# Transposed activations split straight out of PSUM in four places, the norm of twelve heads moved, and the last chunk of the attention output projection taken piece by piece

## The reference, cut to what matters

```python
# first block: attention (differential and latent heads), then a gated convolution FFN
x = x + g1 * (_merge_heads(o_da, o_mla, subln_w, lambda_init) @ w_o)      # 256x2048 @ 2048x2048
h2 = _modulate(_rmsnorm(x, norm2_w), sh2, s2)
x = x + g2 * _conv_ffn(h2, w_up, conv_w, conv_b, w_down)
x = _rmsnorm(x, final_w)
# second block, layer 0: 16 delta-rule heads and 8 windowed heads side by side
proj = rmsnorm(x, norm_w[0]) @ hyb_w_in
o_a = gated_delta_chunked(q_a, k_a, v_a, beta, g)                          # 256 x 16 x 128
o_a = o_a * rsqrt(mean(o_a * o_a, -1) + EPS) * dn_norm_w                   # a norm for each head
y_a = o_a.reshape(256, 2048) * silu(az)
y_b = dilated_attention(q_b, k_b, v_b).reshape(256, 1024) * silu(bz)
x = x + concatenate([y_a, y_b], -1) @ hyb_w_out                            # 256x3072 @ 3072x2048
# layer 1: gated short convolution
gate_b, gate_c, u, z = split(rmsnorm(x, norm_w[1]) @ sc_w_in, 4)
x = x + (gate_b * causal_conv(gate_c * u) * silu(z)) @ sc_w_out
return rmsnorm(x, final_norm_w)
```

## Time and profile before

| | us |
|---|---|
| median of 3 runs | 3053.97 (3048.46 to 3054.05) |
| profiled execution | 3045.87 |
| its span | 3044.0 |
| PE busy | 2877.8 (95%) |
| DVE busy | 1813.1 (60%) |
| ACT busy | 1206.1 (40%) |
| POOL busy | 174.5 (6%) |

### The profile page before, as it was taken

How to read it: one execution, slowest core, us unless ns; L and a number is a source line. 1 busy time by engine, 2 the same in 40 slices (tenths; PEclk the granted TensorE clock), 3 DMA queues, 4 the chain that set the end, 5 groups by cost and what they waited for, 6 DMA issues and landing times.

```text
span 3044.0 us, 35020 instructions
## 1 busy us (share of the span) xinstructions
PE 2877.8 (95%) x13848; PEld 2353.2 (77%) x13848; DVE 1813.1 (60%) x2037; ACT 1206.1 (40%) x1210; POOL 174.5 (6%) x344
## 2 busy tenths in 40 slices
PE   6899998899999999998999999989689999999998
PEld 3597865677888888887877888878677888888887
DVE  2486777775565545565555668957754554455554
ACT  2232226444544334354344434424334344344333
POOL 0000314000000000000000000026200000000000
PEclk9999999999999999999899999999899999999999
DMA  9698974574654565556357767674146454655554
GB/s 393 240 335 284 339 266 143 197 274 149 207 183 168 196 219 177 193 170 192 136 173 257 226 222 234 207 229 117 46 142 199 167 193 161 212 193 193 175 168 155
DMA packets 348289, 618.60 MB, mean 203 GB/s; under 512 B 51808, under 2 KB 102640, under 8 KB 340864
## 3 DMA queue, kind: packets, MB, share of 16 engines
q1 hardware_dynamic: 311280, 583.88, 57.0%
q10 hardware_dynamic: 36880, 32.94, 3.2%
HBM read 587.76 MB, written 29.00 MB: 203 GB/s over the span
## 4 chain that ended last, share of the span: by engine, by line
PE 81%; DVE 10%; DMA 3%; ACT 2%; issue 1%; SPq 1%; POOL 1%; ACTq 0%; DVEq 0%; POOLq 0%
PE ps L309 21%; PE ps L311 20%; PE ps L310 20%; DVE w_lo L271 3%; PE ps L1098 3%; PE ps L1100 3%; PE ps L1099 3%; DVE upd L2435 1%; PE ps L1380 1%; ACT w_hi L264 1%; PE ps L692 1%; DMA g_row<-in_w_ada 1%; DVE w_lo L869 1%; PE ps L415 1%; PE ps L2733 1%
## 5 line engine op out<-in xcount | busy, mean ns | idle before, releaser
L271 DVE TENSOR_TENSOR w_lo<-raw,w_hi 128x2048 fp32r<-128x2048 f32 (+3 forms) x428 | 892.5, 2094 | 695.1 <-ACT w_hi L264 693.8
L264 ACT ACTIVATE w_hi<-raw 128x2048 fp32r<-128x2048 f32 (+3 forms) x428 | 745.0, 1753 | 751.2 <-PE ps L311 664.6
L309 PE MATMUL ps<-w_hi,a_hi 128*128 128x512 f32 (+1 forms) x2272 | 891.0, 392 | 17.8 <-DVE a_lo L731 7.5
L311 PE MATMUL ps<-w_hi,a_lo 128*128 128x512 f32 (+1 forms) x2272 | 884.5, 389 | 0.0
L310 PE MATMUL ps<-w_lo,a_hi 128*128 128x512 f32 (+1 forms) x2272 | 884.0, 389 | 0.0
L309 PEld LDWEIGHTS ps<-w_hi,a_hi 128*128 128x128 f32 x2272 | 430.2, 189 | 110.4 <-DVE a_lo L731 9.2
L311 PEld LDWEIGHTS ps<-w_hi,a_lo 128*128 128x128 f32 x2272 | 430.1, 189 | 88.8
L310 PEld LDWEIGHTS ps<-w_lo,a_hi 128*128 128x128 f32 x2272 | 430.4, 189 | 85.7
L309 PE MATMUL ps<-w_hi,b_hi 128*128 128x512 f32 x764 | 300.0, 393 | 12.7 <-DVE w_lo L271 7.6
L310 PE MATMUL ps<-w_lo,b_hi 128*128 128x512 f32 x764 | 298.6, 391 | 0.0
L311 PE MATMUL ps<-w_hi,b_lo 128*128 128x512 f32 x764 | 298.6, 391 | 0.0
(11 more groups left out here) (352 smaller groups left out, 2948.1 us busy)
## 6 DMA issues: line engine op xcount, KB each, us to landing
raw<-in_hyb_w_in SPq DMA_DIRECT2D x96, 1024.0 KB, 5.5
raw<-in_sc_w_in SPq DMA_DIRECT2D x96, 1024.0 KB, 5.2
raw<-in_w_up SPq DMA_DIRECT2D x88, 1024.0 KB, 5.1
raw<-in_pack_ada SPq DMA_DIRECT2D x96, 512.0 KB, 5.8
raw<-in_w_down SPq DMA_DIRECT2D x48, 768.0 KB, 4.4
raw<-in_w_in SPq DMA_DIRECT2D x24, 1024.0 KB, 6.9
raw<-in_hyb_w_out SPq DMA_DIRECT2D x32, 768.0 KB, 4.5
raw<-in_sc_w_out SPq DMA_DIRECT2D x32, 768.0 KB, 4.5
```

What stands on the lines that cost most here:

```text
L264: nc.scalar.activation(w_hi[s][:, 0:n_k, 0:ncols], raw[s][:, 0:n_k, 0:ncols], ACT.Copy).then_inc(sem("hi_done"), 1)
L271: nc.vector.tensor_tensor(w_lo[s][:, 0:n_k, 0:ncols], raw[s][:, 0:n_k, 0:ncols], w_hi[s][:, 0:n_k, 0:ncols].bitcast(F32), ALU.subtract).th ...
L309: nc.tensor.matmul(o, h, w_hi[s][:, k, 0:ncols], start=kt == 0, stop=False)
L311: last = nc.tensor.matmul(o, l, w_hi[s][:, k, 0:ncols], start=False, stop=kt == L.groups[-1][0] + L.groups[-1][1] - 1)
```

## The change

1. In the flips `mix`, `n3`, `mix2` and `n4` the copy to SBUF is gone. ACT makes the high part from the PSUM bank with the scale, DVE the low part from the same bank with the scale (one multiply-subtract). `mix`, `n3` and `n4` use four banks (4 to 7), `mix2` two. PE may write a bank again when the low part is made. `n2`, `h` and `lat` stay.
2. `flip_hooks` always flips only what the next piece needs.
3. The splits of `mix` stand between the weight splits of WO instead of ahead of or behind them; those of `mix2` pairs 3 to 11 between the weight splits of HO.
4. The last chunk of WO is no longer taken by token tile. Both tiles' residuals come after the chunk; DVE splits two pieces of the FFN's weights ahead of them.
5. The joint stage: `out_sum` of the third group moves from the end of slot 15 to the end of slot 13; the root over the first twelve heads goes behind slot 13's exponential on ACT, its reciprocal and the scalings of eight heads to the end of slot 14 on DVE, the scaling of four more to the end of slot 15. Only the last four heads keep their place after the slots. The flips of `mix2` pairs 0 and 1 go ahead of the last transpose of the slots, pair 2 ahead of the last product, and the three early weight splits of HO lie between them.
6. One set of squares writes its unused result to SBUF, since it would lie in a flip's bank.

```diff
@@ tile_done
-            if t == 0:
-                eng.wait_ge(sem("tile_done"), 1 + (WO, DOWN[1], HO, SO).index(L))
+            if t == 0 and L is not WO:
+                eng.wait_ge(sem("tile_done"), 1 + (DOWN[1], HO, SO).index(L))
@@
+        FLIP_BANKS = {"mix": 4, "n3": 4, "mix2": 2, "n4": 4}
@@ flip_pair
-            if j >= 2:
-                pe.wait_ge(sem("flip_f"), flips_before(name) + j - 1)
+            n_banks = FLIP_BANKS[name] if name in FLIP_BANKS else 2
+            if j >= n_banks and name in FLIP_BANKS:
+                pe.wait_ge(sem("flip_lo"), flips_before(name) + j - n_banks + 1)
+            elif j >= n_banks:
+                pe.wait_ge(sem("flip_f"), copies_before(name) + j - 1)
@@ flip_hooks
-                until(n_pairs if g >= RING - 1 else pairs_for(g + 1))
+                until(pairs_for(g + 1))
@@
+        def flip_hi(act, name, pairs, scale, hi):
+            for j in pairs:
+                act.wait_ge(sem("flip_t"), flips_before(name) + j + 1)
+                for k in [slice(0, 2)] if name in ("mix", "mix2") else [slice(0, 1), slice(1, 2)]:
+                    last = nc.scalar.activation(hi[:, 2 * j + k.start:2 * j + k.stop, :], flipped_pair(name, j)[:, k, :], ACT.Copy,
+                                                scale=scale(2 * j + k.start))
+                last.then_inc(sem("flip_hi"), 1)
+        def flip_lo(dve, name, pairs, scale, hi, lo):
+            for j in pairs:
+                dve.wait_ge(sem("flip_hi"), flips_before(name) + j + 1)
+                for k in [slice(0, 2)] if name in ("mix", "mix2") else [slice(0, 1), slice(1, 2)]:
+                    kt = slice(2 * j + k.start, 2 * j + k.stop)
+                    last = nc.vector.scalar_tensor_tensor(lo[:, kt, :], flipped_pair(name, j)[:, k, :], scale(kt.start),
+                                                          hi[:, kt, :].bitcast(F32), ALU.mult, ALU.subtract)
+                last.then_inc(sem("flip_lo"), 1)
@@ wo_pe
-                matmul_chunk(pe, WO, n, WO.c0 + n, [mix], hooks=hooks if n == 0 else {}, by_tile=n == 3)
+                matmul_chunk(pe, WO, n, WO.c0 + n, [mix], hooks=hooks if n == 0 else {})
@@ wo_act
+                hooks = {"end": lambda: x_squares(act, "n2", WO, n - 1)} if n else {
+                    "end": lambda: flip_hi(act, "mix", (4, 5), mix_scale, b_hi)}
+                if n == 1:
+                    hooks[1] = lambda: flip_hi(act, "mix", (6, 7), mix_scale, b_hi)
@@ wo_dve
-                         "end": lambda: adds(6)} if n else {"end": lambda: adds(0, 8)}
+                         "end": lambda: adds(6)} if n else {
+                    "end": lambda: (flip_lo(dve, "mix", (4, 5), mix_scale, b_hi, b_lo), adds(0, 4),
+                                    flip_lo(dve, "mix", (6, 7), mix_scale, b_hi, b_lo), adds(4, 4))}
@@ joint_pe, after the slots
+            pe.wait_ge(sem("sw_masked"), N_UNIT)
+            mix2_flip(pe, 0)
+            mix2_flip(pe, 1)
             sw_wflip(pe, N_UNIT - 1)
+            mix2_flip(pe, 2)
             sw_pv(pe, N_UNIT - 1)
+            pe.wait_ge(sem("dl_out"), 2 * SLOTS)
+            pe.wait_ge(sem("dl_state"), 2 * SLOTS)
@@ joint_act
+                if s == SLOTS - 1:
+                    act.wait_ge(sem("dl_o"), 2 * SLOTS)
+                    presplit(split_hi, act, HO, 0, 1)
                 sw_exp(act, s)
+                if s == SLOTS - 3:
+                    out_root(act, PAIRS - 1, slice(0, DN_V - CT))
+            flip_hi(act, "mix2", (0, 1), mix2_scale, b_hi)
             sw_wT(act, N_UNIT - 1)
-            act.wait_ge(sem("dl_o"), 2 * SLOTS)
+            presplit(split_hi, act, HO, 1, 2)
+            flip_hi(act, "mix2", (2,), mix2_scale, b_hi)
             act.wait_ge(sem("sw_sc"), N_UNIT)
-            presplit(split_hi, act, HO)
-            act.wait_ge(sem("out_dve"), PAIRS)
-            nc.scalar.activation(ss_a[:], ss_a[:], ACT.Sqrt, ...)
+            presplit(split_hi, act, HO, 2, 3)
+            out_root(act, 2 * PAIRS - 1, slice(DN_V - CT, DN_V))
@@ joint_dve
-                if n == 3 and k:
+                if n == (1 if k == PAIRS - 1 else 3) and k:
                     out_sum(dve, k - 1)
+                if s == SLOTS - 2:
+                    out_factor(dve, chain, 4, 2 * PAIRS - 2, slice(0, DN_V - CT))
+                    out_scale(dve, 0)
+                    out_scale(dve, 1)
+                if s == SLOTS - 1:
+                    out_scale(dve, 2)
             sw_out(dve, N_UNIT - 2)
+            flip_lo(dve, "mix2", (0,), mix2_scale, b_hi, b_lo)
             sw_weights(dve, chain, N_UNIT - 1)
+            flip_lo(dve, "mix2", (1,), mix2_scale, b_hi, b_lo)
+            presplit(split_lo, dve, HO, 0, 1)
+            flip_lo(dve, "mix2", (2,), mix2_scale, b_hi, b_lo)
             sw_out(dve, N_UNIT - 1)
-            presplit(split_lo, dve, HO)
+            presplit(split_lo, dve, HO, 1, 2)
             out_sum(dve, PAIRS - 1)
-            ... (one reciprocal and four scalings)
+            presplit(split_lo, dve, HO, 2, 3)
+            out_factor(dve, chain, 5, 2 * PAIRS, slice(DN_V - CT, DN_V))
+            out_scale(dve, PAIRS - 1)
@@ HO: pairs ahead of which weight piece their splits stand
+        MIX2_FIRST, MIX2_NEXT, MIX2_LAST = (0, 1, 2), {4: (3, 4), 5: (5,), 6: (6, 7), 7: (8,), "end": (9, 10)}, (11,)
@@ scalar queue
-            presplit(split_hi, act, WO)
-            flip_act(act, "mix", KT // 2, b_hi)
+            for g in range(3):
+                presplit(split_hi, act, WO, g, g + 1)
+                if g < 2:
+                    flip_hi(act, "mix", (2 * g, 2 * g + 1), mix_scale, b_hi)
             wo_act(act)
-            x_squares(act, "n2", WO, 3, [0])
             presplit(split_hi, act, UP[0])
-            x_squares(act, "n2", WO, 3, [1])
+            x_squares(act, "n2", WO, 3)
@@ vector queue
-            presplit(split_lo, dve, WO)
-            flip_dve(dve, "mix", ...)
+            for g in range(3):
+                presplit(split_lo, dve, WO, g, g + 1)
+                if g < 2:
+                    flip_lo(dve, "mix", (2 * g, 2 * g + 1), mix_scale, b_hi, b_lo)
             wo_dve(dve, chain)
+            presplit(split_lo, dve, UP[0], 0, 2)
             residual_tile(dve, chain, WO, 3, 0)
-            presplit(split_lo, dve, UP[0], 0, 2)
             residual_tile(dve, chain, WO, 3, 1)
```

More of the change, by code:

```diff
@@ L604, in build_program, with copies_before @@
                  "mix2": MIX_KT // 2, "n4": KT // 2}
+        FLIP_BANKS = {"mix": 4, "n3": 4, "mix2": 2, "n4": 4}
         def flips_before(name):
             return sum(list(FLIPS.values())[:list(FLIPS).index(name)])
+        def copies_before(name):
+            return sum(FLIPS[k] for k in list(FLIPS)[:list(FLIPS).index(name)] if k not in FLIP_BANKS)
         def wait_rms(eng, name):
@@ L699, in flip_pe, with flip_hooks @@
                 flip_pair(pe, name, src, right, j)
-        def flip_hooks(pe, L, name, src, right, first_wait, ready=None):
+        def flip_hooks(pe, L, name, src, right, first_wait, ready=None, first=0):
             n_pairs = FLIPS[name]
-            flipped = [0]
+            flipped = [first]
             def until(n):
```

90 lines of the change are left out of this document (56 added, 34 removed).

## The result

The changed kernel takes 3000.9 us against 3051.9 beside it (medians of four executions each), a ratio of 0.9834 with the interval [0.9817, 0.9851]. Over the whole study there are 72 executions of the kernel before (besides its first profiled one), 3044.2 to 3059.7 us with the median 3051.7, and 14 of the changed one, 2996.0 to 3007.5 with the median 3001.2: 50.5 us less.

A forecast was written before the change was run, and what follows sets the result against it. PE was taken as the bound (81% of the span), gains possible only where it stands still: 15.1 + 3.1 + 2.4 + 23.4 = 44.0 us, so 3045.87 becomes 3001.9, or 3010 at the median; range 3003 to 3021.

The forecast's parts named there:

- the scaling from the profiled execution to the median: Whole kernel: profiled 3045.87 lay 0.27% under the median 3053.97, so 3001.9 was scaled to 3009.9, taken as 3010 us.
- the sum of 44.0: Whole kernel: gains of 15.1 in WO, 3.1 at `n3`, 2.4 at `n4` and 23.4 at HO, in us.
- WO's start: First output projection: PE's first product at about 568.5, 7.2 us earlier; with the first chunk's waits gone, 10.9.
- the last chunk's order: WO's last chunk: taking both tiles in turn removes the fourth piece's wait and slow passes behind the waits, 4.2 us.
- The tiles' order: Behind WO's last chunk: tile 0's residual and squares hide behind the gate row's sum; without that cover about 1.6 us.
- Norm three: Flip `n3`: about 1.0 us at the start, 0.68 at each of two pieces, some 0.7 at the fourth; 3.1 us gained.
- Norm four: Flip `n4`: about 1.0 us at the start and 0.68 at each of the next two pieces; 2.4 us gained.
- Slot 14: Joint stage: a sum put at the end of slot 13 lengthens DVE's loop; slot 14 longer by 1.2 us.
- slot 15: Joint stage: a reciprocal and two scalings at the end of slot 14 lengthen slot 15 by 2.6 us.
- HO's first product: Second output projection: first piece can start at 2190.4 instead of 2202.33, 12 us earlier in relation to slot 12.
- The chunk: HO's first chunk: takes 42.1 us, ending at 2232.5 instead of about 2256.0; gain 23.4 us with the earlier start.
- The rivals' conditions: DMA limits WO: 3018, 9%; GpSimd and clock at joint stage: 3018, 12%; splits queue behind flips: 3066, 4%; little effect: 3013.

The follow-up runs named there:

- the by-tile variant: Changed kernel with WO's last chunk multiplied by token tile again, residuals, squares and next weight splits in old order: median 3003.7 us over nine executions.
- the one profile with these slots at full clock: Profile of the changed kernel with norms three and four turned in two banks and copied by VectorE first, as before: median 3006.79 us (four executions).

## Why the prediction missed

**The step that failed is the scaling from the profiled execution to the median.** For the profiled execution it had 3001.9; it took 3000.65. The last step carried the 8.1 us by which the median of three runs lay above the profiled execution over to the new kernel (3001.9 became 3009.9). They did not carry over: the changed kernel's median lies only 0.6 us above its first profile. Of the 8.1, 2.3 us were the draw of those three runs (the median of 72 is 3051.7, not 3054.0). The other 5.8 were an unusually quick execution: 68 of 72 took longer, and the five other profiles have 10 to 32 us more at half clock.

By stage means the change is worth 49.3 us, by the pair of first profiles 45.2. Of the 4.1 between, 1.0 lie in the first projection and 0.7 in the second. There the usual execution of the kernel before loses more to waits and half clock than the first profile did, and the change takes both away: in the first projection 3 to 6 us at half clock became none, from slot 15's mask to norm four's diagonal 27 to 31 became 0 to 4. Another 2.3 lie from norm three to slot 13, 0.5 behind norm four and -0.4 elsewhere. In the 2.3 the first profile of the kernel before was lucky: the changed kernel stands there at half clock as long as the usual execution before (42 to 48 us against 41 to 49), so the change did not remove it. Why one execution gets less of it than another is open. The forecast called the spread "some 3 us"; it is over 10.

Against the stage means the sum of 44.0 itself is 5.3 us short: 2.1 in the first projection with its start, 0.9 at norm two, 2.3 from slot 13 to norm four, 0.2 behind it, and -0.2 from norm three to slot 13. That it met the profiled execution within 1.3 us is in part luck, since on the pair of first profiles its misses cancel: 1.1 too little in the first projection, 1.3 at norm two and 1.6 from slot 13 on, against 2.5 too much at norm three and 0.2 at norm four.

The other steps, on the first pair of profiles, where not said otherwise:

- WO's start: 7.5 in relation to the turnings' own start, forecast 7.2. In the chunks 8.3 against 7.9 (3.7 and 4.2). How they are shared was wrong: the last chunk's order is worth 2.2 us (104.09 to 101.89; 1.8 to 4.9 against the six profiles) where the first chunk stalls and none where it doesn't, since the by-tile variant has no wait at the fourth piece; the splits are worth the rest, 6.1, or all 8.3 alone.
- The tiles' order costs nothing: right, hidden behind the gate row's sum. The 5.5 us that the forecast read from the product's end to the diagonal are 4.9 in both kernels.
- Not forecast: 1.3 us at norm two (0.9 by the stage means), whose turnings run at full clock in two of the three profiles of the changed kernel.
- Norm three 2.6 to its fourth piece (forecast 3.1): of 1.0 at its first product only 0.2 came, because the 32 turnings ran at half clock (6.53 us) and TensorE itself was the bound. Then some 1.7 was lost in the half-clock stretch behind, 17.1 us long against 13.7. That is the draw of these two executions: it is 13.7 or 20.5 us long in the other profiles of the kernel before, and by the stage means 2.9 us are gained up to slot 13. Norm four 3.4 to its third piece (forecast 2.4), of which 1.2 was lost by the end.
- Slot 14 +1.1 (forecast 1.2), slot 15 +4.25 (forecast 2.6): the two scalings took 2.36 as priced; the other 1.6 is TensorE's. VectorE waited for its products 0.78 and 1.71 us there, 0.26 and 0.73 a slot before, while 3.4 us of the slot ran at half clock. In the one profile with these slots at full clock it took 9.76 us, 2.6 more than before, just as forecast. GpSimd held the third scaling as forecast (2.37), the root's table loads of 1.28 lay ahead of ScalarE's waits. The Trainium skill ("ScalarE: Activation LUTs", What ACT_TABLE_LOAD costs) counts a drain with each; the trace decides for the row, a load of 1.28 right behind the instruction ahead of it.
- HO's first product 12.3 earlier against 11.9, two misses that cancel: the slots came 1.6 later than forecast, but from the last transpose to the product it took 2.4 us, not the 4.2 of the forecast, whose terms (0.7, 2.0 and 1.2, which add up to 3.9) are those of half clock. The chunk 41.05 against 42.1, the gain 25.0 against 23.4.

The rivals' conditions did not come: TensorE waited 0.6 us in all ahead of the products of these projections, and ran at full clock from 2172 to the chunk's end.

## What to carry to other kernels

A sum made on one profiled execution is a difference; subtract it from nothing but a typical execution, and first ask how much of the kernel's scatter sits beside the waits that the change removes, since that part goes too. Where executions scatter by 10 us, four of them can't price a term of 4: profile a variant and compare the one stage, which in the first projection repeated within 0.02 us. Short work for an engine inside a loop costs nothing only if it is put where that engine waits: with the twelve heads' sum, root and scalings in other places of the same slots the median fell by 5.5 us (3001.2 to 2995.7), of which the slots show 1.8 us apart from the clock.

## What was not expected of the hardware

- VectorE's multiply-subtract of 128x512 out of PSUM took 0.73 to 0.75 us with a scale per partition and 0.69 without, two of 128x256 0.88; ScalarE's copy of a bank with a scale per partition 0.68 in place of 0.60. Beside GpSimd's pass the mask, which reads one input from PSUM, kept its 0.96 us (at 2163.38), while the scaling with both inputs in SBUF took 2.37 instead of 1.18.
- An identity product of 128x128 in float32 took 0.23 us in the wait of norm three; with 36 of them there the granted clock from 1420 to 1430 us was 1.00 instead of 0.62. But a stretch of 14 to 21 us at half clock in the middle of unbroken products, beginning 33 to 41 us behind that norm's diagonal, stands in every profile, with or without them.
- The same program's mean clock ranged from 0.976 to 0.981, and its time over 15.5 us.
